# RWKV-7 tiles of a hybrid decoder: moving the next tile's key norm, the output's squares and half of the masked products within the tile

## The chip, the cores and the metric

The kernel runs on one core of a Trainium2 chip. The metric is the device time of one execution in microseconds (us): the median of several executions. Profiles are taken from one further execution, and their times are counted from the start of its span.

## The reference, cut to what matters

One layer of a decoder over 1,072 tokens: 1,040 prompt tokens (16 learned ones ahead of 1,024) and 8 sample sequences of 4 tokens. A projection feeds four token mixers (HGRN2, RWKV-7, GLA, mLSTM) and four gates; then come a branch projection, a gated sum, an output projection and an MLP. The change lies in the RWKV-7 mixer alone:

```python
kk = _heads(k * p['rwkv_k_k'])
kk = kk / jnp.maximum(jnp.linalg.norm(kk, axis=-1, keepdims=True), 1e-12)
# per token, per head (4 heads of 64):
sa = einsum('bhvk,bhk->bhv', s, kk)
s = s * exp(lw)[:, :, None, :] - sa[..., None] * (kk * a)[:, :, None, :] + v[..., None] * k[:, :, None, :]
y = einsum('bhvk,bhk->bhv', s, r)
# then a layer norm of y over each head's 64 values, a bonus term and a gate
```

## The kernel before, in words

Work is staged: mLSTM, then HGRN2 with GLA, then RWKV, then the branch projection, the output projection and the MLP. The 1,072 tokens make 8 tiles of 128 and a last one of 48 (16 prompt tokens and the samples). In each of the three mixer stages TensorE has a second task beside the tile's own matrices: it streams columns of the input projection that a later stage needs. That stream is a Python generator, `stream_pair`, and `steps(work, k)` takes k pieces of it. A piece is six matmuls (lines L450 to L452). A tile has 24 pieces, four to a group; after each fourth piece ScalarE can evacuate the group from PSUM (`evacs`, `stream_out`, recorded at L501; for every third group a copy of weights at L495 follows). The placing of the pieces among the tile's own matmuls is the order written out by hand: they are to keep TensorE busy while VectorE and ScalarE work on the tile.

An RWKV tile (`rw_tile`, written once for each engine; each engine follows its own order and meets the others at semaphores) goes like this:

- TensorE makes the products of the keys and receptances with each other (L1037 to L1039, semaphore `rw_s`), then takes three pieces of the stream and waits for `rw_t`.
- VectorE meanwhile starts the inverse of a triangular matrix. It selects the first level for `ti` (L2054), multiplies four PSUM banks by the causal mask into `pb` and `pk` (L2059, four instructions; `pk` are the products with the keys) and selects the first level for `tt` (L2063), which gives `rw_t`.
- Six more levels follow. In each one TensorE multiplies (L1049), ScalarE copies the result (L1449), TensorE multiplies twice more (L1055, L1059) and VectorE selects (L2072); two pieces of the stream lie in each level. At level 1 TensorE also turns the keys and values into PSUM banks 2 and 3, which held the products for `pk`.
- Between the levels the next tile is prepared. ScalarE scales the shifted columns (L1382) and makes gates and the squares of the keys (L1405); VectorE mixes, and makes the key scale and the bonus terms (`rw_kp`, ending in L1980); TensorE sums the squares over each head at level 6 (`rw_heads`, L1020, semaphore `rw_hs`).
- After the levels come right-hand sides (`rw_rhs`, copied by ScalarE at L1466), the solution (L1086, copied at L1470), the outputs (L1098 and L1105, semaphore `o_done`) and the state update. TensorE then takes three pieces and waits for `o_normed`.
- The output stage. VectorE centres the output (L2093 to L2097, semaphore `rw_yc`); ScalarE evacuates one group, then squares the centred output (L1475); VectorE sums the squares (L2133). ScalarE then makes the reciprocal root (L441, L443). VectorE, in between, normalises the next tile's keys (`rw_norm`: L1986 to L1992, of which L1988 is a reciprocal), and after that multiplies the output (L2137, semaphore `o_normed`). TensorE turns it (L1133), takes the remaining four pieces and starts the next tile, which waits for VectorE's `rw_rc` (L2005).
- The square root that the key norm needs (L1409) and the decays' exponentials (L1415 to L1418) are one ScalarE function, `rw_decay`, called after the copy at L1470. A root and an exponential each need a load of ScalarE's function table (ACT_TABLE_LOAD at L1409 and at L446).

Of the kernel before, what the change touches and what calls it, by code (L numbers as in the profile page):

```python
# [8 lines left out]
ALU = mybir.AluOpType  # L9
# [5 lines left out]
P = 128  # L15
# [43 lines left out]
def constants():  # L59
# [35 lines left out]


SEMAPHORES = """
    act_back act_hi act_parts act_spilled0 act_spilled1 act_sq act_step act_used banks_free0 banks_free1
    chunk_done0 chunk_done1 chunk_loaded0 chunk_loaded1 consts consts_rest conv_ready conv_sent dn_ready down0
    down1 down_used0 down_used1 dve_step gl_att gl_b gl_done gl_gates gl_ke gl_kready gl_lf gl_qb gl_qe gl_qk  # L100
# [38 lines left out]
def build(nc, A, OUT, fcols, ucols, fdim, udim):  # L139
    ctx = ExitStack()  # L140
    with ctx:
# [11 lines left out]
        def S(name):  # L153
            return sems[name]
# [10 lines left out]
        def PS(b, lo=0, hi=512):  # L165
            return PSt[:, b * 512 + lo:b * 512 + hi]
# [278 lines left out]
        def exp_ln_table(e):  # L445
            e.preload_act_table_set("natural_log_exp_and_others")  # L446
# [38 lines left out]
        def steps(work, k):  # L485
            for _ in range(k):
                next(work, None)
# [323 lines left out]
        def _(e):  # L811
# [217 lines left out]
            def rw_tile(n, w, work, w_next, last_tile=False):  # L1029
# [8 lines left out]
                    e.matmul(PS(2 + h % 2, g * 2 * w, (g + 1) * 2 * w)[0:w], RC[r, 4 + g, 0:w], rhs, start=True, stop=True)  # L1038
                    last = e.matmul(PS(4 + h % 2, g * w, g * w + w)[0:w], RC[r, g, 0:w], RC[r, 6 + g, 0:w], start=True, stop=True)  # L1039
                last.then_inc(S("rw_s"), 1)  # L1040
                steps(work, 3)
                tt, ti, m1 = (x.rearrange("p h t -> p (h t)") for x in (RTT, RTI, RM1))
                pb = RPB.rearrange("p h k t -> p (h k t)")
                pk = RPK.rearrange("p h k t -> p (h k t)")
# [1 line left out]
                for l in range(1, nlev):  # L1046
                    lh, m = levels[l], w // 2
                    for h in range(4):
                        last = e.matmul(PS(4, h * m, h * m + m)[0:w], pb[0:w, 2 * h * w:2 * h * w + w],  # L1049
                                        half(ti[0:w, h * w:h * w + w], lh, False), start=True, stop=True)  # L1050
                    last.then_inc(S("rw_m"), 1)
                    steps(work, 1)
                    e.wait_ge(S("rw_m1"), n * 6 + l)
                    for h in range(4):
                        last = e.matmul(PS(0, h * m, h * m + m)[0:w], m1[0:w, h * w:h * w + w],  # L1055
                                        half(tt[0:w, h * w:h * w + w], lh, True), start=True, stop=True)
                    last.then_inc(S("rw_n"), 1)
                    for h in range(4):
                        last = e.matmul(PS(1, h * m, h * m + m)[0:w], tt[0:w, h * w:h * w + w],  # L1059
                                        half(m1[0:w, h * w:h * w + w], lh, False), start=True, stop=True)  # L1060
                    last.then_inc(S("rw_n"), 1)
                    if l == 1:
                        for j in range(4):
                            e.transpose(PS(2, j * P, j * P + P)[0:w], RC[:, 4 + j, 0:w], ident)
                        for j in range(2):
                            last = e.transpose(PS(3, j * P, j * P + P)[0:w], RZS[:, 4 + j, 0:w], ident)
                        last.then_inc(S("k_turned"), 1)
                    if l == 4 and w_next:
                        rw_lora(n + 1, w_next)
                    if l == 6 and w_next:  # L1070
                        rw_heads(n + 1, w_next, RKQ, "rw_kkq", 2, "rw_hs")
                    steps(work, 1)
                    e.wait_ge(S("rw_t"), n * 14 + 2 + 2 * l)
# [123 lines left out]
        def _(e):  # L1197
# [205 lines left out]
            def rw_square(m, w):  # L1403
                e.wait_ge(S("rw_kk"), m + 1)
                e.activation(RKQ[:, :, 0:w], RKK[:, :, 0:w], ACT.Square).then_inc(S("rw_kkq"), 1)  # L1405

            def rw_decay(m, w):
                e.wait_ge(S("rw_hs"), m + 1)
                e.activation(RRN[:, :, 0:w], PS(2, 0, 2 * w).rearrange("p (g t) -> p g t", g=2),  # L1409
                             ACT.Sqrt).then_inc(S("rw_nrm"), 1)  # L1410
                exp_ln_table(e)
                e.wait_ge(S("rw_wl"), m + 1)
                if w == P:
                    at = bass.ds(m, 1)
                    e.activation(REC[:, :, at], RCS[:, :, at], ACT.Exp, scale=-DECAY)  # L1415
                e.activation(RE3[:, :, 0:w], RWX[:, :, 0:w], ACT.Exp, scale=-DECAY)
                e.activation(RE1[:, :, 0:w], RWL[:, :, 0:w], ACT.Exp, scale=-DECAY)
                e.activation(RE2[:, :, 0:w], RWL[:, :, 0:w], ACT.Exp, scale=DECAY).then_inc(S("rw_e"), 1)  # L1418
# [9 lines left out]
            rw_square(0, P)  # L1428
            stream_out(e, J_RW0, 0, 2)
            stream_out(e, J_RW0, 1, 0)  # L1430
            rw_decay(0, P)
            stream_out(e, J_RW0, 1, 1)
            rw_bonus(0, P)
# [2 lines left out]
            def rw_tile(n, w, j, w_next):  # L1436
                last_tile = w < P
                turns = iter([(u, g) for u in range(2) for g in range(3)])

                def evacs(k):  # L1440
                    for _ in range(k):
                        stream_out(e, j, *next(turns), more=not last_tile)
                levels = LHALVES if last_tile else HALVES
                nlev = len(levels)
                m1 = RM1.rearrange("p h t -> p (h t)")[0:w, 0:4 * w].rearrange("p (h t) -> p h t", h=4)
                for l in range(1, nlev):
                    e.wait_ge(S("rw_m"), n * 6 + l)
                    h = levels[l]
                    e.activation(half(m1, h, False), PS(4, 0, 2 * w)[0:w].rearrange("p (a n t) -> p a n t", a=4, t=h),  # L1449
                                 ACT.Copy).then_inc(S("rw_m1"), 1)  # L1450
                    if l % 2:
                        evacs(1)
                    if l == 1:
                        e.wait_ge(S("k_turned"), n + (RW_N + 1))
                        e.activation(RKB[0:w], PS(2)[0:w], ACT.Copy)
                        e.activation(RV[0:w], PS(3, 0, 256)[0:w], ACT.Copy).then_inc(S("k_back"), 1)
                        if w_next:
                            e.wait_ge(S("rw_bv"), n + 1)
                            rw_scaled(n + 1, w_next)
                    if w_next and l == 3:  # L1460
                        rw_tanh(n + 1, w_next)
                    if w_next and l == 5:
                        rw_gates(n + 1, w_next)
                        rw_square(n + 1, w_next)
                e.wait_ge(S("rw_rhs"), n + 1)
                e.activation(RRS[0:w], PS(4, 0, 256)[0:w], ACT.Copy).then_inc(S("rw_r"), 1)  # L1466
                if not last_tile:
                    evacs(1)
                e.wait_ge(S("rw_u"), n + 1)
                e.activation(RUS[0:w], PS(5, 0, 256)[0:w], ACT.Copy).then_inc(S("rw_us"), 1)  # L1470
                if w_next:
                    rw_decay(n + 1, w_next)
                evacs(2 if last_tile else 1)
                e.wait_ge(S("rw_yc"), n + 1)
                e.activation(RSQ[0:w], RY[0:w], ACT.Square, scale=0.125).then_inc(S("o_sq"), 1)  # L1475
                e.wait_ge(S("o_ms"), n + (RW_N + 1))
                rstd(e, st, RMS_[0:w, 3], RMS_[0:w, 2], LN_EPS).then_inc(S("o_rs"), 1)
                if w_next:
                    rw_bonus(n + 1, w_next)
                evacs(2 if last_tile else 1)  # L1480
# [84 lines left out]
        def _(e):  # L1565
# [458 lines left out]
            def rw_tile(n, w, j, w_next):  # L2024
# [28 lines left out]
                for i in range(2):  # L2053
                    ins = e.copy_predicated(ti[:, i:4:2, :], mkt, PS(4 + i, 0, 2 * w)[0:w].rearrange("p (h t) -> p h t", h=2))  # L2054
                ins.then_inc(S("rw_t"), 1)
                for i in range(2):
                    for (dst, bank) in ((pb, 0), (pk, 2)):
                        dst = dst.rearrange("p (i j c) -> p i j c", i=2, j=2)[:, :, i, :]
                        e.tensor_tensor(dst, PS(bank + i, 0, 4 * w)[0:w].rearrange("p (i c) -> p i c", i=2),  # L2059
                                        bc(cm.unsqueeze(1), [w, 2, 2 * w]), ALU.mult)  # L2060
                for i in range(2):
                    src = PS(i, 0, 4 * w)[0:w].rearrange("p (i k t) -> p i k t", i=2, k=2)[:, :, 0, :]
                    ins = e.copy_predicated(tt[:, i:4:2, :], mk, src)  # L2063
                ins.then_inc(S("rw_t"), 1)
                levels = LHALVES if last_tile else HALVES
                for l, h in list(enumerate(levels))[1:]:
                    for q, (dst, bank, mk) in enumerate(((tt, 0, "ll" if last_tile else "lv"), (ti, 1, "llt" if last_tile else "lvt"))):
# [18 lines left out]
                    if w_next and l == 6:  # L2086
                        weights_lo(e, j + 4, 0)
                        rw_kp(n + 1, w_next)

                y = PS(1, 0, 256).rearrange("p (h c) -> p h c", h=4)[0:w]  # L2090
                r = [RMS_[0:w, k] for k in range(4)]
# [39 lines left out]
                    st.did(ins)  # L2131
                e.wait_ge(S("o_sq"), n + (RW_N + 1))
                e.tensor_reduce(r[2], RSQ[0:w], AX.X, ALU.add).then_inc(S("o_ms"), 1)  # L2133
                if w_next:
                    rw_norm(n + 1, w_next)
                e.wait_ge(S("o_rs"), n + (RW_N + 1))
                e.tensor_tensor(RY[0:w], RY[0:w], bc(r[3].unsqueeze(2), [w, 4, 64]), ALU.mult).then_inc(S("o_normed"), 1)  # L2137
                e.wait_ge(S("o_turned"), n + (RW_N + 1))
# [250 lines left out]
```

## Time and profile before

| | us |
|---|---|
| median of 3 executions | 2546.67 |
| lowest and highest | 2542.06, 2553.62 |
| profiled execution, its own time | 2545.37 |
| its span | 2543.8 |
| eight full RWKV tiles in it | 918.6 to 1406.2 |

In the rows further down an engine's busy time is that of its recorded instructions. PE is TensorE's matmuls, PEld its weight loads, DVE is VectorE, ACT is ScalarE. AR is the one large SBUF arena in which all tiles of a stage lie, and PS is PSUM. A releaser (after `<-`) is the instruction that ended the idle time ahead of an instruction.

### The profile page before, as it was taken

The numbers are of one execution on the slowest core, as the hardware profiler recorded it, in microseconds if no ns is written. First come the engines' busy times: TensorE is split into PE (matmuls) and PEld (weight loads), VectorE is DVE, ScalarE is ACT, GpSimd is POOL, SyncE is SP. The second block draws the span as 40 slices with busy tenths as digits, with TensorE's granted clock in tenths as the row PEclk, the third lists the DMA queues.
The fourth block names the chain that finished last, engine by engine and source line by source line (L and its number), as shares of the span: only waits on it lengthen the run. The fifth ranks groups of instructions, "written<-read, shape, count | busy, mean of one in ns | idle before, by whom it ended". The sixth has DMA issues, their size and how long they took to land.

```text
span 2543.8 us, 34492 instructions
## 1 busy us (share of the span) xinstructions
PE 2269.4 (89%) x13669; PEld 2156.7 (85%) x13669; DVE 1176.0 (46%) x1973; ACT 675.8 (27%) x1071; POOL 183.5 (7%) x339
## 2 busy tenths in 40 slices
PE   4998988799999789999998868899999997999996
PEld 3977778789898688888888867899999997999995
DVE  5423331566666444444444357652222224555565
ACT  5222112323232043333333044101100102333342
POOL 1000011131222100000000021100000001000000
PEclk8988899899899889999999879999999998999998
DMA  4111125212121221111111055412111224111112
GB/s 162 43 51 51 40 44 120 91 50 75 58 68 58 73 84 44 42 42 45 42 42 41 16 194 180 138 44 108 48 42 41 62 89 181 42 41 41 41 41 86
DMA packets 82632, 178.25 MB, mean 70 GB/s; under 512 B 10464, under 2 KB 50096, under 8 KB 82320
## 3 DMA queue, kind: packets, MB, share of 16 engines
q1 hardware_dynamic: 67056, 123.35, 15.5%
q0 software_dynamic: 15488, 54.13, 6.5%
q8 instruction: 37, 0.61, 0.1%
q14 instruction: 19, 0.16, 0.0%
q10 hardware_dynamic: 32, 0.01, 0.0%
HBM read 129.43 MB, written 48.02 MB: 70 GB/s over the span
## 4 chain that ended last, share of the span: by engine, by line
PE 75%; DVE 11%; ACT 5%; DMA 4%; issue 3%; POOL 1%; POOLq 0%; DVEq 0%; ACTq 0%; SPq 0%
PE PS L450 20%; PE PS L451 19%; PE PS L452 19%; PE PS L941 2%; DMA AR<-zrows 2%; PE PS L1059 2%; PE PS L1055 2%; PE PS L1049 2%; DMA orows<-AR 1%; DVE AR L1824 1%; DVE AR L2186 1%; DVE AR L2059 1%; DVE AR L1822 1%; ACT AR L1352 1%; ACT AR L1382 1%
## 5 line engine op out<-in xcount | busy, mean ns | idle before, releaser
L450 PE MATMUL PS<-HT_parts,W_parts 128*128 128x358 f32 x1440 | 531.7, 369 | 14.9 <-ACT AR L501 10.9
L451 PE MATMUL PS<-OT_parts,W_parts 128*128 128x358 f32 x1440 | 494.4, 343 | 0.0
L452 PE MATMUL PS<-HT_parts,W_parts 128*128 128x358 f32 x1440 | 492.3, 342 | 0.0
L450 PEld LDWEIGHTS PS<-HT_parts,W_parts 128*128 128x128 f32 x1440 | 294.4, 204 | 25.4 <-ACT AR L501 11.4
L451 PEld LDWEIGHTS PS<-OT_parts,W_parts 128*128 128x128 f32 x1440 | 293.3, 204 | 2.2
L452 PEld LDWEIGHTS PS<-HT_parts,W_parts 128*128 128x128 f32 x1440 | 291.4, 202 | 0.0
L450 PE MATMUL PS<-ACT_parts,CF_parts 128*128 128x358 f32 x768 | 255.6, 333 | 26.5 <-DVE ACT_parts L532 16.0
L450 PE MATMUL PS<-HN_parts,CF_parts 128*128 128x358 f32 x768 | 251.3, 327 | 4.7 <-DVE OT_parts L532 4.7
L452 PE MATMUL PS<-HN_parts,RING_parts 128*128 128x358 f32 x768 | 250.9, 327 | 0.0
L452 PE MATMUL PS<-ACT_parts,RING_parts 128*128 128x358 f32 x768 | 250.8, 327 | 0.0
L451 PE MATMUL PS<-OT_parts,CF_parts 128*128 128x358 f32 x768 | 250.7, 326 | 0.0
L501 ACT ACTIVATE AR<-PS 128x358 f32<-128x358 f32 x162 | 75.9, 470 | 566.7 <-PE PS L452 553.0
L450 PEld LDWEIGHTS PS<-ACT_parts,CF_parts 128*128 128x128 f32 x768 | 145.2, 189 | 35.7 <-issue 30.8
L1548 ACT ACTIVATE ACT_parts<-AR 128x1074 fp32r<-128x1074 f32 x96 | 105.8, 1103 | 199.5 <-PE PS L452 183.8
L450 PEld LDWEIGHTS PS<-HN_parts,CF_parts 128*128 128x128 f32 x768 | 145.2, 189 | 5.0 <-DVE OT_parts L532 5.0
L452 PEld LDWEIGHTS PS<-HN_parts,RING_parts 128*128 128x128 f32 x768 | 145.2, 189 | 0.0
L452 PEld LDWEIGHTS PS<-ACT_parts,RING_parts 128*128 128x128 f32 x768 | 145.1, 189 | 0.0
L451 PEld LDWEIGHTS PS<-OT_parts,CF_parts 128*128 128x128 f32 x768 | 144.7, 188 | 0.0
L2072 DVE COPY_PREDICATED AR<-CU,PS 128x256 f32<-128x256 uint8 (+1 forms) x102 | 42.9, 478 | 184.7 <-PE PS L1059 177.3
L507 DVE TENSOR_TENSOR W_parts<-RING,W_parts 128x1024 fp32r<-128x1024 f32 x60 | 73.9, 1231 | 116.2 <-ACT W_parts L495 90.8
L451 PE MATMUL PS<-ACT_parts,CF_parts 128*128 128x358 f32 x384 | 126.6, 330 | 0.0
L451 PE MATMUL PS<-CF_parts 128*128 128x358 f32 x384 | 125.2, 326 | 0.0
(385 smaller groups left out, 3696.3 us busy)
## 6 DMA issues: line engine op xcount, KB each, us to landing
RING<-in_w_all SPq DMA_DIRECT2D x132, 512.0 KB, 3.7
zrows<-AR SPq DMA_DIRECT2D x162, 179.0 KB, 1.9
AR<-zrows POOLq DMA_DIRECT2D x32, 537.0 KB, 3.8
AR<-zrows SPq DMA_DIRECT2D x8, 640.0 KB, 4.5
AR<-in_xT SPq DMA_DIRECT2D x8, 537.0 KB, 7.1
HT<-in_xT POOLq DMA_DIRECT2D x8, 537.0 KB, 6.8
residual<-HT POOLq DMA_DIRECT2D x8, 537.0 KB, 6.5
acts<-AR POOLq DMA_DIRECT2D x8, 537.0 KB, 3.3
```

The costliest lines, as they stand in the source:

```text
L450: e.matmul(out, whi, xhi, start=first, stop=False)
L451: e.matmul(out, whi, xlo, start=False, stop=False)
L452: return e.matmul(out, wlo, xhi, start=False, stop=last)
L501: e.activation(ZS[:, g], PS(6 + (u + g) % 2, 0, GRP), func).then_inc(S("gt_free"), 1)
L507: e.tensor_tensor(RLO_R[:, u], RING[:, u], RHI_R[:, u].bitcast(F32), ALU.subtract).then_inc(S(f"split{u}"), 1)
L941: last = e.matmul(PS(3 * (l % 2), lo * m, hi * m)[0:w], x[:, g, l, 0:w], GQB[:, l % 2, lo * m:hi * m], start=True, stop=True)
L1049: last = e.matmul(PS(4, h * m, h * m + m)[0:w], pb[0:w, 2 * h * w:2 * h * w + w], half(ti[0:w, h * w:h * w + w], lh, False), start=True, s ...
L1055: last = e.matmul(PS(0, h * m, h * m + m)[0:w], m1[0:w, h * w:h * w + w], half(tt[0:w, h * w:h * w + w], lh, True), start=True, stop=True)
L1059: last = e.matmul(PS(1, h * m, h * m + m)[0:w], tt[0:w, h * w:h * w + w], half(m1[0:w, h * w:h * w + w], lh, False), start=True, stop=True)
L1352: e.activation(x[:, :, 1:hi, :], x[:, :, 1:hi, :], ACT.Exp).then_inc(S("x_exp"), 1)
L1548: e.activation(AHI_R[r % 2], act_row(r), ACT.Copy).then_inc(S("act_hi"), 1)
L2072: e.copy_predicated(dst, bc(mk.unsqueeze(1), dst.shape), PS(bank, 0, 2 * w)[0:w].rearrange("p (a n t) -> p a n t", a=4, t=h)).then_inc(S(" ...
```

## The change

Six edits, all in the RWKV stage:

- On VectorE the four causal products are split: those for `pb` stay ahead of the selection of `tt`, those for `pk` go behind it and count a new semaphore, `rw_pk`. TensorE waits for `rw_pk` at level 1, ahead of the turning of keys and values.
- TensorE takes four pieces of the stream, not three, ahead of the wait for `rw_t`. The tile's total stays 24, so the pieces behind L1133 become three.
- `rw_decay` is split. The root and the load of the exponential's table (`rw_root`) go to level 6 on ScalarE; the exponentials stay.
- On VectorE `rw_norm` of the next tile goes from the output stage to level 6, behind `rw_kp`.
- On ScalarE the squares of the centred output go ahead of that stage's evacuation (in all but the last tile).
- In the prelude the root is called where it was, ahead of the exponentials.

```diff
@@ TensorE, rw_tile
                 last.then_inc(S("rw_s"), 1)
-                steps(work, 3)
+                steps(work, 4)
...
                     if l == 1:
+                        e.wait_ge(S("rw_pk"), n + 1)
                         for j in range(4):
                             e.transpose(PS(2, j * P, j * P + P)[0:w], RC[:, 4 + j, 0:w], ident)
@@ ScalarE
-            def rw_decay(m, w):
+            def rw_root(m, w):
                 e.wait_ge(S("rw_hs"), m + 1)
                 e.activation(RRN[:, :, 0:w], PS(2, 0, 2 * w).rearrange("p (g t) -> p g t", g=2),
                              ACT.Sqrt).then_inc(S("rw_nrm"), 1)
                 exp_ln_table(e)
+
+            def rw_decay(m, w):
                 e.wait_ge(S("rw_wl"), m + 1)
@@ ScalarE, rw_tile
                     if w_next and l == 5:
                         rw_gates(n + 1, w_next)
                         rw_square(n + 1, w_next)
+                    if w_next and l == 6:
+                        rw_root(n + 1, w_next)
...
                 if w_next:
                     rw_decay(n + 1, w_next)
-                evacs(2 if last_tile else 1)
+                if last_tile:
+                    evacs(2)
                 e.wait_ge(S("rw_yc"), n + 1)
                 e.activation(RSQ[0:w], RY[0:w], ACT.Square, scale=0.125).then_inc(S("o_sq"), 1)
+                if not last_tile:
+                    evacs(1)
                 e.wait_ge(S("o_ms"), n + (RW_N + 1))
@@ VectorE, rw_tile
-                for i in range(2):
-                    for (dst, bank) in ((pb, 0), (pk, 2)):
-                        dst = dst.rearrange("p (i j c) -> p i j c", i=2, j=2)[:, :, i, :]
-                        e.tensor_tensor(dst, PS(bank + i, 0, 4 * w)[0:w].rearrange("p (i c) -> p i c", i=2),
-                                        bc(cm.unsqueeze(1), [w, 2, 2 * w]), ALU.mult)
+                def causal(dst, bank):
+                    for i in range(2):
+                        d = dst.rearrange("p (i j c) -> p i j c", i=2, j=2)[:, :, i, :]
+                        ins = e.tensor_tensor(d, PS(bank + i, 0, 4 * w)[0:w].rearrange("p (i c) -> p i c", i=2),
+                                              bc(cm.unsqueeze(1), [w, 2, 2 * w]), ALU.mult)
+                    return ins
+                causal(pb, 0)
                 for i in range(2):
                     src = PS(i, 0, 4 * w)[0:w].rearrange("p (i k t) -> p i k t", i=2, k=2)[:, :, 0, :]
                     ins = e.copy_predicated(tt[:, i:4:2, :], mk, src)
                 ins.then_inc(S("rw_t"), 1)
+                causal(pk, 2).then_inc(S("rw_pk"), 1)
...
                         weights_lo(e, j + 4, 0)
                         rw_kp(n + 1, w_next)
+                        rw_norm(n + 1, w_next)
...
                 e.tensor_reduce(r[2], RSQ[0:w], AX.X, ALU.add).then_inc(S("o_ms"), 1)
-                if w_next:
-                    rw_norm(n + 1, w_next)
                 e.wait_ge(S("o_rs"), n + (RW_N + 1))
```

## Rows read from the trace of the kernel before

**Rows 1.** Windows of two stages: start:end length, busy us of engines, PEclk, DMA
```profile
918.60:1406.20 487.60, 440.77 (x3107) 421.32 (x3105) 213.35 (x564) 164.70 (x375) 0.58 (x1) 0.95 0.14 44
1740.00:2100.00 360.00, 360.00 (x2196) 360.00 (x2195) 96.72 (x91) 33.25 (x31) 3.72 (x7) 1.00 0.17 54
```
**Rows 2.** Waits of PE in the tiles, 980 to 1407: us, times, longest
```profile
PE PS L1133 <- DVE AR L2137: 30.6, 7, 4.6
```
**Rows 3.** Windows inside the third tile, columns as in Rows 1
```profile
1041.28:1102.57 61.29, 55.21 (x389) 52.80 (x389) 27.16 (x70) 20.84 (x47) 0.00 (x0) 0.94 0.14 44
1047.33:1048.31 0.98, 0.01 (x1) 0.00 (x0) 0.93 (x3) 0.00 (x0) 0.00 (x0) 1.00 0.01 4
1048.31:1079.36 31.05, 30.50 (x233) 29.15 (x234) 8.81 (x26) 12.56 (x30) 0.00 (x0) 1.00 0.12 35
1088.12:1091.09 2.97, 2.97 (x19) 2.67 (x17) 0.92 (x4) 0.00 (x0) 0.00 (x0) 1.00 0.00 0
1091.09:1095.65 4.56, 0.00 (x1) 0.01 (x1) 3.56 (x6) 1.55 (x5) 0.00 (x0) 0.87 0.11 40
1095.65:1101.59 5.94, 5.94 (x21) 5.94 (x22) 4.49 (x16) 0.00 (x0) 0.00 (x0) 0.52 0.00 0
```
**Rows 4.** Timeline of VectorE at that tile's start: start, us, line, op
```profile
1045.10 2.48 DVE L2059 TENSOR_TENSOR AR<-PS,CF 128x512 f32<-128x512 f32 x4
1047.49 0.77 DVE L2063 COPY_PREDICATED AR<-CU,PS 128x256 f32<-128x256 uint8 x2
```
**Rows 5.** Timeline of PE and ScalarE from level 6 to the decays
```profile
1078.70 0.66 PE L1020 MATMUL PS<-AR,CF 128*128 128x128 f32 x4
1082.52 1.00 PE L1086 MATMUL PS<-AR 128*128 128x64 f32 x8
1081.73 0.39 ACT L1466 ACTIVATE AR<-PS 128x256 f32<-128x256 f32 x1 [5.23 <-PE PS L1105]
1083.56 0.38 ACT L1470 ACTIVATE AR<-PS 128x256 f32<-128x256 f32 x1 [0.37 <-PE PS L1086]
1083.96 1.28 ACT L1409 ACT_TABLE_LOAD   x1
1085.65 1.28 ACT L446 ACT_TABLE_LOAD   x1
1087.67 0.40 ACT L1418 ACTIVATE AR<-AR 128x256 f32<-128x256 f32 x1
```
**Rows 6.** Timeline of VectorE from level 6 to the end of the output stage
```profile
1081.91 0.62 DVE L1980 SCALAR_TENSOR_TENSOR AR<-AR,CC 128x128 f32<-128x128 f32 x2
1086.82 0.42 DVE L2093 TENSOR_REDUCE AR<-PS 128x4 f32<-128x256 f32 x1 [4.29 <-PE PS L1105]
1087.48 0.42 DVE L2097 TENSOR_TENSOR AR<-PS,AR 128x256 f32<-128x256 f32 x1
1088.46 0.61 DVE L2130 SCALAR_TENSOR_TENSOR AR<-AR 128x128 f32<-128x128 f32 x2
1091.93 0.42 DVE L2133 TENSOR_REDUCE AR<-AR 128x4 f32<-128x256 f32 x1 [2.85 <-ACT AR L1475]
1095.17 0.42 DVE L2137 TENSOR_TENSOR AR<-AR 128x256 f32<-128x256 f32 x1
```
**Rows 7.** Timeline of ScalarE in the output stage
```profile
1091.12 0.47 ACT L501 ACTIVATE AR<-PS 128x358 f32<-128x358 f32 x1 [3.06 <-PE PS L452]
1091.49 0.41 ACT L1475 ACTIVATE AR<-AR 128x256 f32<-128x256 f32 x1
1092.71 0.21 ACT L443 ACTIVATE AR<-AR 128x4 f32<-128x4 f32 x1
```
**Rows 8.** Timeline of VectorE behind L1133, up to the next tile's rw_rc
```profile
1096.38 0.61 DVE L2141 SCALAR_TENSOR_TENSOR AR<-PS,CC,AR 128x128 f32<-128x128 f32 x2 [0.78 <-PE PS L1133]
1098.08 1.42 DVE L2005 TENSOR_TENSOR AR<-AR 128x256 f32<-128x256 f32 x4
```
**Rows 9.** Window from the eighth tile's wait at L1133 to its end, as Rows 1
```profile
1397.16:1406.20 9.04, 5.84 (x27) 5.62 (x26) 5.06 (x21) 1.41 (x5) 0.00 (x0) 0.81 0.06 22
```

More of the change, by code:

```diff
@@ L97 @@
 SEMAPHORES = """
+    rw_pk
     act_back act_hi act_parts act_spilled0 act_spilled1 act_sq act_step act_used banks_free0 banks_free1
@@ L1430, in _ @@
             stream_out(e, J_RW0, 1, 0)
+            rw_root(0, P)
             rw_decay(0, P)
```

## The prediction

> **What bounds the kernel now.** I read the windows of the stages first. In the eight full RWKV tiles TensorE is busy for 440.77 of 487.60 us at a mean granted clock of 0.95, while VectorE is busy for 213 and ScalarE for 165 [rows 1]. So TensorE sets the stage's time, and there are two things to win back: 46.8 us in which it idles, and what the lower clock costs. Next the waits of TensorE: one line holds two thirds of the idle time, L1133 (the turning of the normalised output) waiting for VectorE's L2137, 30.6 us in seven waits, those of the second to the eighth tile [rows 2]. Last the windows inside one tile of 61.29 us. TensorE idles 0.98 us ahead of level 1 and 4.56 us ahead of L1133; then the clock, 1.00 before, reads 0.52 for the next 5.94 us [rows 3]. The two levels are 2.4 and 1.2 GHz. Behind the short idle time the clock stays at 1.00 for 31 us, with TensorE idle for another 0.55 in them [rows 3].
>
> **The unit of work.** A piece of the stream is six matmuls. Three pieces took 2.97 us at full clock [rows 3], so one takes 0.99. The row at low clock holds L1133 and 18 stream matmuls, 5.94 us [rows 3].
>
> **Start of the tile: four pieces, and `pk` behind the selection.** L2063 ended at 1047.49 + 0.77 = 1048.26. Two of the four L2059 (2.48 / 2 = 1.24 us) now follow it, so `rw_t` comes at 1047.02 [rows 4]. TensorE ended its third piece at 1047.33; a fourth keeps it busy until 1048.32, and level 1 starts there, as before, with 1.3 us to spare. One piece of 0.99 us has filled an idle time of 0.98 and is gone from the end of the tile: **0.97 gained**. If `rw_t` came late after all, the 0.98 us idle would stay and the gain be nothing. The new wait for `rw_pk`: the products for `pk` now end where L2063 ended, at 1048.26, when level 1 has only started; the transposes that wait lie behind level 1's own multiplications in TensorE's queue. Cost 0; if that cover were gone, it is at most the 1.24 us, once a tile, with the rest of TensorE's queue behind it.
>
> **Level 6 on ScalarE: the root with two table loads.** It waits for L1020, which ends at 1078.70 + 0.66 = 1079.36. From the start of the first load to that of the second took 1085.65 - 1083.96 = 1.69 us, and the second load 1.28 [rows 5]: done by 1082.33 if the first load stands behind the wait, by 1081.05 if ahead of it. Queued behind it on ScalarE is the copy L1466, whose result TensorE's L1086 needs. It started at 1081.73 before and ended at 1082.12; now it ends at up to 1082.33 + 0.39 = 1082.72, against L1086's start at 1082.52 [rows 5]. Bounds 0 and 0.2; I take **0.1 lost**, the middle.
>
> One rule of the Trainium skill speaks against this edit. The rows show a load of 1.28 us that starts 0.02 us after the copy ahead of it ended, and the second load directly behind the root [rows 5]. The Trainium skill, "ScalarE: Activation LUTs", section "What ACT_TABLE_LOAD costs", puts a drain of about 1.38 us beside each load, some 2.66 us a switch. By that, an estimate from the page, two drains would push L1466 2.76 us further, and TensorE with it. The trace has no such drain here, so the sum goes by the rows.
>
> **Level 6 on VectorE: the key norm.** It follows L1980, which ends at 1082.53, and the root is there by 1081.05. It ran between L2133's end (1092.35) and L2137's start (1095.17), 2.82 us; with its hand-overs I take 2.9, so it ends at about 1085.5. The output stage's first instruction, L2093, could not start before 1086.82, when TensorE's outputs were done [rows 6]. Hidden by 1.3 us of VectorE's waiting; were that cover gone, it would cost up to 2.9 us there.
>
> **The output stage.** The centred output is ready at 1087.90 [rows 6]. ScalarE's exponentials are earlier by the moved 2.97 us, so from 1088.07 to 1085.1 [rows 5], and the squares (0.41 [rows 7]) end at 1088.35. VectorE's state update ends at 1089.07 and the sum of squares at 1089.5 [rows 6]. But ScalarE now stands in the evacuation, with the reciprocal root queued behind it. That group is done with piece 20; as one piece was moved ahead, that is now the second of the three pieces here, at 1088.2 + 1.98 = 1090.2 (0.1 is L1466's delay). The next ScalarE instruction follows the evacuation by 0.37 us (1091.12 to 1091.49 [rows 7]), at 1090.6. From the sum's end (1092.35 [rows 6]) to the end of L443 (1092.92 [rows 7]) took 0.57: 1091.15. L2137 takes 0.42, and TensorE started 0.06 after its end (1095.65): with one more hand-over, L1133 starts at 1091.65. TensorE ends its third piece at 1091.2. It idles 0.46 us where it idled 4.56: **4.10 gained**. Between 0.3 and 0.8 is what the hand-overs leave open.
>
> **The clock.** An idle time of 0.46 us lies below the one of 0.98 behind which the clock stayed at 1.00 [rows 3], so I take it that the low stretch goes. L1133 and three pieces at full clock take 0.45 + 2.97 = 3.42 instead of 5.94: **2.5 gained**. Lower bound 0 (a rival).
>
> **What is late next.** The next tile's first matmul waits for `rw_rc`. L2005 ended at 1098.08 + 1.42 = 1099.50 [rows 8], 3.85 us after L1133's start. At full clock the two transposes are 0.25 shorter: 3.6, against TensorE's 3.42. **0.2 lost.**
>
> **Sum.** A tile: 0.97 - 0.1 + 4.10 + 2.5 - 0.2 = 7.27 us. The first seven tiles are alike (the third stands for them [rows 3]): 50.9. In the eighth the idle time is 9.04 - 5.84 = 3.20, and the clock, 0.81 over these 9.04 us, was low for some 3.4, costing 1.7 [rows 9]; six times 4.56 and this 3.20 make the 30.6 [rows 2]. The tile after it is narrow and its `rw_rc` earlier. 0.97 - 0.1 + 2.74 + 1.7 = 5.3. In the last tile one piece moves from its end to its start: 0, with 1 us either way. Together 56.2: 2545.4 - 56.2 = 2489.2 for the profiled execution, which lay 1.3 below the median. **Forecast 2490.**
>
> **Rivals.**
> - The clock falls all the same (the eighth tile's 3.20 also led to a low stretch [rows 9], and where between 0.98 and 3.20 it begins no row shows). Then 0.97 - 0.1 + 4.10 = 5.0 a tile, nothing for `rw_rc`; seven times 5.0 and 3.6 are 38.6: 2508. Chance 0.12.
> - The loads of tables hold ScalarE longer at level 6 than their rows show. If each took twice its 1.28 us [rows 5], L1466 would end 2.56 later and TensorE's L1086 wait about 2.5 more. A tile gains 4.8, the eighth 2.8: 36.4 in all, 2510. For it speaks nothing in the rows, against it that root and second load follow the first at once. Chance 0.05. The Trainium skill's drains ("ScalarE: Activation LUTs", as above), an estimate from that page, would make it 2512.
> - The key norm is not hidden: the root comes late, from 1083.9 on it delays L2093. If all 2.9 us lay behind `o_done`, the chain would bring L1133 at 1092.9; 1.2 us more a tile: 2500. Chance 0.05.
> - Slower: TensorE's several short idle times in a tile (0.46, 0.2 and those inside the levels) hold the clock low through half of each tile instead of 5.94 us. L1133 and 18 matmuls show the ratio, 5.94 / 3.42 = 1.74; 27 us at low clock hold 11.5 us that full clock would save: 8 x 11.5 above the forecast, 2582. It decides from about 17 low us a tile, where 7.3 x 1.74 / 0.74 eats the gain. Against it: 1.00 right after the 0.98 idle [rows 3], and 1.00 through 360 us without idle time [rows 1], so density alone lowers nothing. Chance 0.03.
> - The change doesn't do what it says: another releaser takes L2137's place and L1133 still starts after 1095: 2546. No chain of the rows adds to that. Chance 0.03.
>
> The forecast has the remaining 0.72. 0.5%, some 13 us, is about what a measurement of this kernel can tell from no change. Faster by more: 0.72 + 0.12 + 0.05 + 0.05 = 0.94; within: 0.03; slower: 0.03. The range runs from the forecast less 10 (the spread of the executions before, 2542 to 2554, and hand-overs shorter than taken) to 2512, which takes in the first three rivals, the highest at 2510.
>
> **What would show it.** In the changed kernel's trace a full tile should take 54 us; TensorE's wait at level 1 be gone; its wait ahead of L1133's counterpart be about 0.5 us, released by the multiplication behind ScalarE's reciprocal root; the granted clock read 1.00 through the tile; a new wait of about 0.2 us stand ahead of the next tile's first products; the reciprocal end before the centring starts. Wrong it would be with a low clock behind L1133, with TensorE waiting for L1466's copy by over 0.5 us, or with the centring waiting for the key norm.

## The result and the profile after

The changed kernel's median is 2490.47 us (2482.79 to 2492.49) against 2548.94 for the kernel before (2542.06 to 2553.62): a ratio of 0.9767, 95% interval 0.9735 to 0.9799. It is faster, by about 58 us. The profiled execution took 2482.79 us, 62.6 less than the one before.

The windows of the stage come first (start:end, length, busy us of PE, PEld, DVE, ACT and POOL, granted clock, DMA share, GB/s): the eight full tiles, the third of them, and its stretch from the turning matmul (now L1135) to its end. (The expectations below call this tile the second.) They answer to [rows 1] and [rows 3]; for the kernel before the same eight tiles, start to start, were 487.35 us.

```profile
916.79:1345.31 428.52, 419.19 (x3105) 401.90 (x3104) 212.15 (x562) 160.07 (x375) 0.58 (x1) 1.00 0.16 50
1024.38:1078.06 53.68, 52.41 (x389) 50.21 (x389) 27.06 (x71) 20.25 (x48) 0.00 (x0) 1.00 0.16 50
1074.40:1078.06 3.66, 3.38 (x21) 3.09 (x21) 2.67 (x10) 0.25 (x1) 0.00 (x0) 1.00 0.13 45
```

A full tile takes 53.68 us instead of 61.29, and the granted clock reads 1.00 all through. The waits of TensorE from the second tile on (total us, times, longest) answer to [rows 2]:

```profile
PE PS L1056 <- ACT AR L1454: 3.3, 6, 0.6
PE PS L1135 <- DVE AR L2150: 3.2, 7, 0.5
PE PS L1038 <- DVE AR L2015: 1.7, 6, 0.3
```

The 30.6 us ahead of the turning have become 3.2. The wait at level 1 is gone; a new one of 0.3 us stands ahead of the next tile's first products (L1038). The wait at level 2 (L1056) is as it was: 3.2 us in six waits in the kernel before.

The timeline of ScalarE in the third tile, from level 6 to the end of the output stage, answers to [rows 5] and [rows 7]:

```profile
1059.42 1.28 ACT L1411 ACT_TABLE_LOAD   x1
1062.29 0.39 ACT L1411 ACTIVATE AR<-PS 128x256 f32<-128x256 f32 x1 [1.59 <-PE PS L1021]
1062.69 1.28 ACT L447 ACT_TABLE_LOAD   x1
1064.61 0.38 ACT L1473 ACTIVATE AR<-PS 128x256 f32<-128x256 f32 x1 [0.63 <-PE PS L1107]
...
1070.82 0.42 ACT L1483 ACTIVATE AR<-AR 128x256 f32<-128x256 f32 x1 [3.00 <-DVE AR L2112]
1072.99 0.47 ACT L502 ACTIVATE AR<-PS 128x358 f32<-128x358 f32 x1 [1.75 <-PE PS L453]
1073.36 0.29 ACT L442 ACTIVATE AR<-AR,CF 128x4 f32<-128x4 f32 x1
```

The first table load ran while the root's input was still being made (L1411's load at 1059.42, the root itself at 1062.29 behind L1021). Both loads were done at 1063.97, and the copy L1473 was not late: it waited for TensorE. In the output stage the squares (L1483) start as soon as the output is centred, and ScalarE then stands in the evacuation until 1073.36, with the reciprocal root queued behind it.

VectorE and TensorE in the same tile answer to [rows 6] and [rows 8]:

```profile
1067.90 0.42 DVE L2002 SCALAR_TENSOR_TENSOR AR<-AR 128x256 f32<-128x256 f32 x1
1069.70 0.42 DVE L2108 TENSOR_REDUCE AR<-PS 128x4 f32<-128x256 f32 x1 [1.37 <-PE PS L1107]
1073.92 0.42 DVE L2150 TENSOR_TENSOR AR<-AR 128x256 f32<-128x256 f32 x1 [1.63 <-ACT AR L444]
```

```profile
1031.34 1.00 PE L1050 MATMUL PS<-AR 128*128 128x64 f32 x8
1070.39 0.61 PE L1021 MATMUL PS<-AR,CF 128*128 128x128 f32 x4
1074.40 0.44 PE L1135 MATMUL PS<-CF,AR 128*128 128x128 f32 x2 [0.45 <-DVE AR L2150]
1078.06 0.70 PE L1038 MATMUL PS<-AR 64*128 64x256 f32 x2 [0.28 <-DVE AR L2015]
```

The key norm ends (L2002) 1.37 us before the centring can start (L2108). Level 1 starts without a wait.

### The profile page after: what moved, and what is told of

Same layout as the page of the kernel before. It is cut to its first block, busy times and chain, and to the rows that moved or that the text cites. A ratio compares the mean times of both kernels' runs of the same rounds, so it can differ in the third digit from the quotient of the medians.

```text
span 2481.2 us, 34492 instructions
## 1 busy us (share of the span) xinstructions
PE 2245.5 (91%) x13669; PEld 2135.1 (86%) x13669; DVE 1175.2 (47%) x1973; ACT 670.7 (27%) x1071; POOL 183.5 (7%) x339
## 4 chain that ended last, share of the span: by engine, by line
PE 77%; DVE 10%; ACT 5%; DMA 4%; issue 3%; POOL 1%; POOLq 0%; DVEq 0%; ACTq 0%; SPq 0%
PE PS L451 20%; PE PS L452 19%; PE PS L453 19%; DMA AR<-zrows 2%; PE PS L942 2%; PE PS L1060 2%; PE PS L1056 2%; PE PS L1050 2%; DMA orows<-AR 1%; DVE AR L1834 1%; DVE AR L2199 1%; DVE AR L1832 1%; ACT AR L1354 1%; ACT AR L1384 1%; PE PS L1107 1%
## 5 line engine op out<-in xcount | busy, mean ns | idle before, releaser
L451 PE MATMUL PS<-HT_parts,W_parts 128*128 128x358 f32 x1440 | 524.0, 364 | 15.3 <-ACT AR L502 11.3
L452 PE MATMUL PS<-OT_parts,W_parts 128*128 128x358 f32 x1440 | 487.3, 338 | 0.0
L453 PE MATMUL PS<-HT_parts,W_parts 128*128 128x358 f32 x1440 | 485.6, 337 | 0.0
L451 PEld LDWEIGHTS PS<-HT_parts,W_parts 128*128 128x128 f32 x1440 | 287.6, 200 | 25.8 <-ACT AR L502 11.8
L452 PEld LDWEIGHTS PS<-OT_parts,W_parts 128*128 128x128 f32 x1440 | 287.1, 199 | 2.3
L453 PEld LDWEIGHTS PS<-HT_parts,W_parts 128*128 128x128 f32 x1440 | 285.7, 198 | 0.0
```

The source lines that it names most:

```text
L451: e.matmul(out, whi, xhi, start=first, stop=False)
L452: e.matmul(out, whi, xlo, start=False, stop=False)
L453: return e.matmul(out, wlo, xhi, start=False, stop=last)
```

## The experiments

Single executions of one kernel scatter by some 10 us (2482.79 to 2492.49 for the changed one), while the eight tiles, from the first one's start to the ninth's, repeat closely: 428.52 and 428.43 us in two profiles of the changed kernel. So small effects are read from the tiles' windows, one line each; the median and its ratio to the kernel before, with the 95% interval in brackets, stand ahead of them. All kernels start from the changed one.

**e1: the key norm back in the output stage.**

```diff
                         rw_kp(n + 1, w_next)
-                        rw_norm(n + 1, w_next)
...
                 e.tensor_reduce(r[2], RSQ[0:w], AX.X, ALU.add).then_inc(S("o_ms"), 1)
+                if w_next:
+                    rw_norm(n + 1, w_next)
```

> The changed kernel with one part undone: the next tile's key norm stands in the output stage again, between the sum of squares and the output's multiplication. Theory (the norm was hidden at level 6 and stands on the chain to the turning matmul here): the sum of squares ends at 1072.28 in the changed kernel's second tile, the norm takes 2.9 us, the multiplication and hand-over 0.47, so the turning starts at 1075.65 instead of 1074.40. TensorE idles about 1.7 us there instead of 0.45 in seven tiles (the eighth has a norm of 96 columns, 1.5 us, about hidden behind the reciprocal root). If an idle time of 1.7 leaves the granted clock at 1.00: 7 x 1.25 = 8.8 us more, 2499. Rival (the clock falls at 1.7 already): another 7 x 2.5 = 17.5 us, 2517, with a clock near 0.5 behind the turning. Rival (the norm cost nothing, ScalarE's order alone was the gain): 2490.

2493.75 us, ratio 0.9785 (0.9748 to 0.9821). Its eight tiles, the wait ahead of the turning, and the stretch behind that wait:

```profile
917.71:1354.37 436.66, 419.05 (x3106) 401.66 (x3105) 211.37 (x563) 160.19 (x375) 0.58 (x1) 1.00 0.16 49
```

```profile
PE PS L1135 <- DVE AR L2151: 10.3, 7, 1.6
```

```profile
1078.80:1082.51 3.71, 3.38 (x20) 3.09 (x21) 2.66 (x10) 0.24 (x1) 0.00 (x0) 1.00 0.00 0
```

8.1 us more than the changed kernel's 428.52, where 8.8 were expected; the idle time is 1.6 and the clock stays at 1.00. The norm was on the chain, and with the rest of the change in place hiding it is worth 8 us.

**e2: the squares back behind the evacuation.**

```diff
-                if last_tile:
-                    evacs(2)
+                evacs(2 if last_tile else 1)
                 e.wait_ge(S("rw_yc"), n + 1)
                 e.activation(RSQ[0:w], RY[0:w], ACT.Square, scale=0.125).then_inc(S("o_sq"), 1)
-                if not last_tile:
-                    evacs(1)
```

> The changed kernel with one part undone: ScalarE evacuates the stream's group first and squares the centred output after it, as before the change. Theory: the evacuation starts at 1072.99 in the changed kernel's second tile, the squares at 1073.36, they end at 1073.77, the sum of squares at 1074.2, the reciprocal root at 1074.8, and the turning starts at 1075.3. TensorE idles about 1.35 us instead of 0.45: 0.9 in eight tiles, 7.2 us more, 2497, clock still 1.00. Rival (the clock falls at 1.35): 2517. Rival (the squares' order is worth nothing once the norm is gone from the stage): 2490.

2493.43 us, ratio 0.98 (0.9774 to 0.9826).

```profile
914.10:1349.82 435.72, 419.16 (x3105) 401.77 (x3104) 212.72 (x563) 160.19 (x375) 0.58 (x1) 1.00 0.16 49
```

7.2 us more in the tiles, as expected, clock 1.00.

**e3: both back.** The two edits above in one kernel.

> The changed kernel with two parts undone: squares behind the evacuation and the key norm in the output stage. Theory: the two add up on one chain, the sum of squares ends at 1074.2, the norm at 1077.1, the turning starts at 1077.6, idle time about 3.65 us in seven tiles and 1.9 in the eighth, so 7 x 3.2 + 1.4 = 23.8 us; and the clock falls behind it as in the kernel before (4.56 idle): 2.5 a tile, 17.5. Together 2531. Rival (no low stretch at 3.65): 2514. Rival (the parts don't add, each hides the other): about 2500.

2515.78 us, ratio 0.9878 (0.9857 to 0.9899). The eight tiles, the fourth tile and the stretch behind a turning; then the waits from the second tile on:

```profile
917.31:1377.93 460.62, 429.46 (x3105) 412.53 (x3105) 212.69 (x563) 160.16 (x375) 0.58 (x1) 0.97 0.15 46
1091.49:1149.48 57.99, 53.88 (x389) 51.76 (x388) 27.17 (x72) 20.27 (x47) 0.00 (x0) 0.97 0.15 46
1086.55:1091.49 4.94, 4.87 (x20) 4.64 (x20) 3.79 (x16) 0.00 (x0) 0.00 (x0) 0.65 0.01 3
```

```profile
PE PS L1135 <- DVE AR L2148: 23.6, 7, 3.6
```

32.1 us more in the tiles: twice the sum of e1 and e2 (15.3). Singly undone, each is half covered by the other engine's chain; together they stand one behind the other, and the idle time grows from 0.45 to 3.57. The clock falls, as expected, but the expected time of 2531 was too high. A tile is 4.31 us longer than the changed kernel's, of which the idle time is 3.12; that leaves 1.2 for the lower clock and the vanished wait of 0.28 together, not the 2.5 that [rows 3] showed behind 4.56 us. The stretch at the lower level was shorter here: a mean of 0.65 over 4.94 us makes some 3.5 us at 1.2 GHz, where 0.52 over 5.94 us made 5.7. Some 8 of the 32.1 us are thus the clock's; the idle times alone make some 24, still more than 15.3. The time and the tiles lie between the theory and the rival that left the clock alone.

**e6: the root back behind the copy of the solution.** The norm stays at level 6.

```diff
-                    if w_next and l == 6:
-                        rw_root(n + 1, w_next)
...
                 if w_next:
+                    rw_root(n + 1, w_next)
                     rw_decay(n + 1, w_next)
```

> The changed kernel with one part undone: the root and its two table loads stand behind the copy of the solution on ScalarE again; the key norm stays at level 6 on VectorE, so VectorE now waits there for the root. Theory: the root ends at 1068.5 in the changed kernel's second tile, the norm at 1071.45, the centring starts 1.75 us late (1071.45 instead of 1069.70), the centred output comes at 1072.5, the state update now lies behind it, the sum of squares ends at 1074.1, the reciprocal root at 1074.7, the turning starts at 1075.2 instead of 1074.40: 0.8 in eight tiles, 6.4 us more, 2497, with VectorE waiting for the root by about 3 us a tile. Rival (the root's place is indifferent, the norm's alone matters): 2490.

2487.11 us, ratio 0.9754 (0.9726 to 0.9781). Its tiles, and a wait of VectorE in its third tile:

```profile
917.78:1351.28 433.50, 419.08 (x3106) 401.78 (x3105) 212.01 (x563) 161.89 (x375) 0.58 (x1) 1.00 0.16 49
```

```profile
DVE AR L1995 <- ACT AR L1411: 3.1, 1, 3.1
```

VectorE waits 3.1 us for the root (L1411), as told. 5.0 us more in the tiles, 6.4 expected: in the eighth tile, with its narrow norm, the wait ahead of the turning didn't change. The whole time can't tell this from the changed kernel. So the norm that is not hidden costs 0.7 us a tile when it comes about in this way (an idle time of 1.17 instead of 0.45), less than the 1.2 of the prediction's rival, and the root's new place is what keeps it away.

**e4: the products for `pk` back ahead of the selection.**

```diff
                 causal(pb, 0)
+                causal(pk, 2).then_inc(S("rw_pk"), 1)
...
                 ins.then_inc(S("rw_t"), 1)
-                causal(pk, 2).then_inc(S("rw_pk"), 1)
```

> The changed kernel with one part undone: the masked products with the keys stand ahead of the first level's selection again; TensorE still takes four pieces there. Theory (the fourth piece covers the whole of the later selection): the selection comes 1.24 us later, at 1031.47 in the changed kernel's second tile, and TensorE's four pieces end at 1031.5: no wait, 2490. Rival (the reordering is what removed the idle time at level 1): up to 1.2 us a tile, 10 us more, 2500.

2485.64 us, ratio 0.9763 (0.9731 to 0.9796). Its tiles, and level 1 in the third tile on VectorE and TensorE:

```profile
917.01:1347.50 430.49, 421.29 (x3106) 401.73 (x3105) 212.26 (x563) 160.08 (x375) 0.58 (x1) 1.00 0.16 49
```

```profile
1031.40 0.76 DVE L2077 COPY_PREDICATED AR<-CU,PS 128x256 f32<-128x256 uint8 x2
1031.91 0.32 PE L453 MATMUL PS<-HT_parts,W_parts 128*128 128x358 f32 x1
1032.22 1.11 PE L1050 MATMUL PS<-AR 128*128 128x64 f32 x8
```

2.0 us more in the tiles, 0.25 in each, though no wait is recorded at level 1. The selection ends at 1032.16, when the last stream matmul is still recorded as busy (to 1032.23); in a stream that isn't held up the next matmul starts 0.17 us after the one before it, and here it starts 0.31 after. Its own eight matmuls then take 1.11 us, 0.11 more than in the changed kernel. The fourth piece covers nearly all of the late selection; the reordering is worth the last 0.25 us a tile.

**e5: three pieces ahead of level 1, `pk` behind the selection.**

```diff
-                steps(work, 4)
+                steps(work, 3)
```

> The changed kernel with one part undone: TensorE takes three pieces ahead of level 1, so four stand behind the turning; the masked products with the keys stay behind the selection. Theory: no wait at level 1 (the selection is there at 1030.23, the third piece ends at about 1030.5), but the group that ScalarE evacuates in the output stage is now finished by the third piece there, not the second, so the reciprocal root comes 0.99 later and TensorE idles 1.45 us ahead of the turning instead of 0.45; four pieces behind the turning cover the wait for the next tile's rows, 0.28. Net 0.7 in eight tiles, 5.7 us more, 2496. Rival (pieces only change places, nothing is lost): 2490. Rival (the idle time of 0.98 at level 1 comes back too): 2504.

2490.89 us, ratio 0.9776 (0.9744 to 0.9809). Its tiles and its waits from the second tile on:

```profile
917.75:1352.57 434.82, 419.28 (x3106) 401.71 (x3105) 212.99 (x563) 163.84 (x375) 0.58 (x1) 1.00 0.16 49
```

```profile
PE PS L1135 <- DVE AR L2150: 10.1, 7, 1.5
```

6.3 us more in the tiles (5.7 expected). The cost lies at the turning, where ScalarE's evacuation now waits for the third piece: 1.44 us of idle time in a tile instead of 0.45, less what the wait at L1038, which is gone, had cost. Level 1 has no wait. With `pk` behind the selection, the fourth piece is worth its 0.8 us a tile through the group that ScalarE evacuates in the output stage.

**e9 and e10: the clock by itself.** Reciprocals whose results nobody uses delay the multiplication in seven tiles; e10 has the third one, of 128x128, as well.

```diff
+        SPARE = a.take(t=P)
...
                 e.tensor_reduce(r[2], RSQ[0:w], AX.X, ALU.add).then_inc(S("o_ms"), 1)
+                if w_next == P:
+                    e.reciprocal(RRN, RKK)
+                    e.reciprocal(RKQ, RKK)
+                    e.reciprocal(SPARE, RKK[:, 0])
```

> A measurement of the clock alone: the changed kernel with two more reciprocals of 128x256 (1.75 us each) on VectorE between the sum of squares and the output's multiplication, in seven tiles; their results are used by nothing. The turning starts about 1.8 us later, so TensorE idles about 2.25 us ahead of it. If the clock stays at 1.00 there: 7 x 1.8 = 12.6 us more, 2503. If it falls as in the kernel before: another 17.5, 2520, with a granted clock near 0.5 behind the turning. The first theory goes by the idle time of 0.98 that cost no clock, the rival by those of 3.20 and 4.56 that did.

> As the kernel with two more reciprocals, and a third one of 128x128 (0.95 us) behind them: TensorE idles about 3.2 us ahead of the turning, as in the eighth tile of the kernel before. 7 x 2.7 = 19 us more if the clock stays: 2509. If it falls for about 3.4 us a tile as in that eighth tile: another 1.7 a tile, 2521.

2496.78 us, ratio 0.9793 (0.9764 to 0.9821), and 2508.39 us, ratio 0.9838 (0.9809 to 0.9867). For e9 the turnings of its second and third tile, and the windows of these two tiles (the third window line is e9's stretch behind the second turning):

```profile
1023.81 0.44 PE L1135 MATMUL PS<-CF,AR 128*128 128x128 f32 x2 [1.94 <-DVE AR L2153]
1080.17 0.44 PE L1135 MATMUL PS<-CF,AR 128*128 128x128 f32 x2 [1.94 <-DVE AR L2153]
```

```profile
972.29:1028.59 56.30, 53.81 (x388) 51.51 (x388) 31.26 (x78) 20.03 (x47) 0.00 (x0) 0.97 0.15 48
1028.59:1083.82 55.23, 52.47 (x389) 50.26 (x388) 29.19 (x69) 20.54 (x48) 0.00 (x0) 1.00 0.16 49
1023.80:1031.80 8.00, 7.99 (x45) 7.36 (x46) 5.71 (x17) 1.42 (x2) 0.00 (x0) 0.79 0.18 47
```

For e10 two neighbouring tiles, both behind an idle time of 2.75:

```profile
976.53:1033.69 57.16, 53.87 (x390) 51.73 (x389) 31.17 (x75) 20.30 (x47) 0.00 (x0) 0.97 0.15 47
1033.69:1089.67 55.98, 52.40 (x389) 50.20 (x389) 29.95 (x70) 20.54 (x48) 0.00 (x0) 1.00 0.15 48
```

The idle times came out shorter than expected (1.94 and 2.75, not 2.25 and 3.2). In e9 two of the seven tiles lost the clock, in e10 five: equal idle times, unequal outcomes. So neither theory holds as it was put, that all tiles do the same. A tile that loses the clock is 1.1 to 1.2 us longer (56.30 against 55.23, 57.16 against 55.98). The eight tiles took 441.33 and 450.79 us, 12.8 and 22.3 more than the changed kernel's: the longer idle times of seven tiles make 10.4 and 16.1 of that, the lost clock nearly all the rest. What sets a tile that loses the clock apart from one that keeps it, no run here shows.

**e7, e8 and e11: on from the changed kernel.** e7 puts the output stage's evacuation behind the reciprocal root; e8 in addition puts ScalarE's scaling behind level 2's copy; e11 in addition puts the next tile's bonus sums behind the turning.

```diff
-                if not last_tile:
-                    evacs(1)
                 e.wait_ge(S("o_ms"), n + (RW_N + 1))
                 rstd(e, st, RMS_[0:w, 3], RMS_[0:w, 2], LN_EPS).then_inc(S("o_rs"), 1)
                 if w_next:
                     rw_bonus(n + 1, w_next)
-                evacs(2 if last_tile else 1)
+                evacs(2)
... e8
-                        if w_next:
-                            e.wait_ge(S("rw_bv"), n + 1)
-                            rw_scaled(n + 1, w_next)
+                    if w_next and l == 2:
+                        e.wait_ge(S("rw_bv"), n + 1)
+                        rw_scaled(n + 1, w_next)
... e11
-                if w_next:
-                    rw_heads(n + 1, w_next, RBX, "rw_bx", 3, "rw_bon")
                 steps(work, 3)
...
                 last.then_inc(S("o_turned"), 1)
+                if w_next:
+                    rw_heads(n + 1, w_next, RBX, "rw_bx", 3, "rw_bon")
                 rest(work)
```

> The changed kernel with one more move: on ScalarE the output stage's evacuation goes behind the reciprocal root and the bonus copy (both of the last two evacuations stand together there). Theory (the 0.45 us left at the turning is ScalarE standing in that evacuation): the reciprocal root starts when the sum of squares is there, at 1072.3 in the changed kernel's second tile, not at 1073.36, the multiplication ends at 1073.3, before TensorE's third piece (1073.96): no wait at the turning. 0.45 in eight tiles, 3.6 us less, 2487. The wait of 0.28 for the next tile's rows stays. Rival (the wait comes back in another place, at the PSUM bank that is evacuated later, or at the next tile's rows): 2490.

> As the kernel with the late evacuation, and ScalarE's scaling of the next tile's columns goes from level 1 to level 2, behind that level's copy. Theory (TensorE's wait of 0.55 us at level 2 in seven tiles is that copy standing behind the scaling, 2.4 us): the copy starts as soon as the level's first product is there, the wait goes, 7 x 0.55 = 3.9 us less than the kernel with the late evacuation alone, 2483. Rival (the scaling then holds up VectorE's mixing, and the selections behind it, or ScalarE's copy of level 3): 2487 or more.

> As the kernel with the late evacuation and the later scaling, and TensorE sums the next tile's bonus terms (four small matmuls, 0.45 us) behind the turning of the output instead of ahead of the three pieces. Theory (the wait of 0.25 us for the next tile's rows, about 0.2 more with the restart of the stream, is what is left between the tiles): the turning starts up to 0.45 earlier and the four matmuls cover the wait behind it, so a full tile takes 51.8 to 52.0 us instead of 52.20, seven times: 1.5 to 3 us less. Rival (the turning then waits for the output's multiplication, which ended 0.48 before it): 52.2, no change. Rival (VectorE, whose copies and weight split follow the rows, becomes the one that the first selection waits for): 52.2, no change.

> The changed kernel unaltered, on the same chip as the kernel with all three further moves, to compare the two: eight full tiles took 428.5 us here and should take 51.9 x 7 + 51.5 = 415 there. If the difference in the tiles reaches the whole time, this kernel is about 13 us slower; if the rest of the execution takes it up, they agree.

2478.23 us (ratio 0.9738, 0.9711 to 0.9765), 2476.19 (0.9721, 0.9697 to 0.9745) and 2472.98 (0.9712, 0.9696 to 0.9728); the changed kernel beside e11, on the same chip, 2488.70 (0.9772, 0.9756 to 0.9788). The eight tiles of e7, e8, e11 and of the changed kernel in that last comparison (e12):

```profile
918.33:1341.48 423.15, 417.67 (x3105) 402.41 (x3104) 212.08 (x563) 160.32 (x375) 0.58 (x1) 1.00 0.16 50
```

```profile
911.46:1328.73 417.27, 415.62 (x3105) 402.88 (x3104) 212.05 (x563) 161.22 (x375) 0.58 (x1) 1.00 0.16 51
```

```profile
914.73:1330.26 415.53, 415.39 (x3105) 401.98 (x3104) 212.31 (x563) 162.11 (x375) 0.58 (x1) 1.00 0.16 51
```

```profile
915.65:1344.08 428.43, 419.18 (x3106) 401.87 (x3105) 211.92 (x562) 160.11 (x375) 0.58 (x1) 1.00 0.16 50
```

Each of the three does what it was to do: e7 takes 5.4 us from the tiles, e8 another 5.9, e11 another 1.7. In e11 TensorE is recorded busy for 415.39 of 415.53 us, and its whole time is 15.7 us below the changed kernel's, of which the tiles make 12.9. It beats both kernels. e7 and e8 gave more than the recorded idle time that they removed: 5.4 for 8 x 0.45, 5.9 for 7 x 0.55. That is e4's observation again, 0.2 to 0.3 us a wait.

## Why the prediction was right, point by point

The forecast was 2490 with a range of 2480 to 2512; the measured median is 2490.47. The nearness is partly luck: the profiled execution came out at 2482.79, where the sum had 2489.2. The steps, per full tile:

| Stretch of the tile | before | after | gained | predicted |
|---|---|---|---|---|
| start to level 1 (one piece of 0.99 more after) | 7.10 | 6.96 | 1.13 | 0.97 |
| level 1 to the end of the bonus sums | 39.81 | 39.66 | 0.15 | -0.1 |
| from there to the turning | 7.53 | 3.40 | 4.13 | 4.10 |
| turning to the next tile (one piece of 0.99 less after) | 6.85 | 3.66 | 2.20 | 2.3 |
| tile | 61.29 | 53.68 | 7.61 | 7.27 |

The columns are differences of the starts in [rows 3], in the rows of after above (the bonus sums end at 1070.39 + 0.61 = 1071.00) and in these three rows of the kernel before, whose tile starts 0.07 us ahead of the window in [rows 3]:

```profile
1041.21 0.70 PE L1037 MATMUL PS<-AR 64*128 64x256 f32 x2
1048.31 1.10 PE L1049 MATMUL PS<-AR 128*128 128x64 f32 x8 [0.98 <-DVE AR L2063]
1102.50 0.70 PE L1037 MATMUL PS<-AR 64*128 64x256 f32 x2
```

- **Start of the tile.** Right, and a little more than told: 1.13 here and 0.15 behind it, where 0.97 and nothing were counted for it. That fits what e4 shows, a wait that costs 0.25 us more than is recorded; level 1 took 1.10 us behind the wait of the kernel before and takes 1.00 now. e4 and e5 divide the credit: with four pieces the late selection would cost only 0.25, and with the early selection three pieces bring no wait to level 1 but 1.0 to the turning. Each edit covers for the other, as the two moved in the output stage do.
- **The root.** The term of 0.1 was mis-sized; it is the lower bound, 0. The first table load doesn't stand behind the root's wait, as the rows above show. The rival of longer loads falls with the same rows: the second load starts 0.01 us after the root has ended. The drain that the Trainium skill gives ("ScalarE: Activation LUTs", "What ACT_TABLE_LOAD costs") shows neither there nor as a delay of L1473.
- **The key norm.** Hidden, with 1.37 us to spare (1.3 predicted). e1 prices it at 1.2 us a tile on its own, e3 at far more with the squares behind the evacuation. e6 shows the rival in which it isn't hidden.
- **The output stage.** The idle time is 0.45 (0.46 predicted), and what released it is what was named: ScalarE standing in the evacuation. e7 removes that and the wait goes.
- **The clock.** 1.00 through all eight tiles. The gain of 2.5 was right for this pair of kernels, because the one before ran some 5.7 us of a tile at 1.2 GHz. It was not a property of a low stretch as such: e3, e9 and e10 lost 1.1 to 1.2 a time, net of the wait behind it, with shorter ones. The rival in which the clock still falls didn't come: in the eight tiles the runs show that only behind idle times of 1.94 us and more, and here it was 0.45.
- **What is late next.** The wait for the next tile's rows was 0.28 where 0.2 was told.
- **The slower rival** has no support: the changed kernel's tiles have several short idle times each (0.45 at the turning, 0.28 at the next tile, up to 0.6 at level 2), and the clock reads 1.00 all through. It reads so without any idle time too, with 415.39 of 415.53 us busy in e11.
- **The sum.** 58.8 us in the eight tiles (487.35 - 428.52) where 56.2 were predicted: 7.25 to 8.00 in each of the first seven (7.27 told) and 5.33 in the eighth (5.3 told). The rest of the 62.6 between the two profiled executions is 2.1 us ahead of the first tile, where nothing changed, and 1.7 behind the eighth. Neither is clear of what differs from profile to profile: with the code ahead of it unaltered, the first tile starts between 911.46 and 919.16 us in the runs above, and what follows the eighth tile took 1135.9 us in the changed kernel here and 1138.3 in e12, the same kernel.

## What to carry to other kernels

Where one engine's queue holds the tile's chain and work for a later purpose, follow the chain to its last link and ask of each instruction queued ahead of it whether it could stand in an earlier idle time of that engine; here that was a norm on VectorE and an evacuation on ScalarE. Price such moves together: undone singly they cost 8.1 and 7.2 us, undone together 32.1, of which the lower clock is some 8. And count pieces of filler by which group they finish, not only by the time they fill, since another engine may wait for exactly that group.

## What the runs showed of the hardware that I had not expected

- The clock's fall isn't settled by the length of the idle time alone. Ahead of the turning, TensorE idled 1.63 us or less in e1, e2, e4, e5, e6 and the changed kernel, and kept 1.00 in each of the eight tiles; at 1.94 two tiles of seven lost it, at 2.21 (e3's eighth tile) the single one kept it, at 2.75 five of seven lost it, at 3.57 (e3) all seven. At 4.56 it fell in all seven tiles and cost 2.5 us, with some 5.7 us at 1.2 GHz; at 1.94 to 3.57 it cost some 1.1 to 1.2, net of the wait of 0.28 that goes with it, with some 3.5 us at 1.2 GHz in e3.
- A wait costs the stream 0.2 to 0.3 us more than the idle time that is recorded: 0.25 a tile in e4 with none recorded, 5.4 us in e7 for 3.6 recorded. e4's rows show where it goes. A stream matmul is recorded as busy for 0.32 us though the next one starts 0.17 us after it, so the first 0.15 us of a wait lie inside its record; and the eight matmuls behind the wait took 1.11 us instead of 1.00.
- The table load of `rw_root` ran ahead of the semaphore wait of the root that needs it, though the code writes that wait first: the load at 1059.42, the root at 1062.29, behind L1021.
